# A decoder block's projections as seven half-matrix products per group instead of eight

## What is computed

```
h = rms_norm(x, g_mix)                                   # 256 x 1024
qa, ka, va, z, beta, a, qd, kd, vd, gate_a, gate_b = split(h @ w_in)   # mostly 1024 columns each
oa = gated_delta_rule(l2(silu(conv(qa))), l2(silu(conv(ka))), silu(conv(va)), ...)
oa = rms_norm(oa, g_delta_out) * silu(z)
od = rms_norm(diff_attention(rms(qd), rms(kd), vd, ...), g_subln) * (1 - lam_init)
x1 = x + (sigmoid(gate_a + b) * oa + sigmoid(gate_b + b) * od) @ w_o
out = x1 + experts(rms_norm(x1), top 4 of 32; w_up 1024 x 2048, w_down 1024 x 1024 each)
```

## Time and profile before

| | |
|---|---|
| median of 3 runs | 1276.09 us (1275.90 to 1276.17) |
| span of the profiled execution | 1273.7 us |
| PE busy | 1229.8 us, 97% |
| DVE busy | 373.2 us, 29% |
| ACT busy | 284.8 us, 22% |
| granted TensorE clock | 0.999 of full |
| moved by DMA | 451.94 MB, mean 355 GB/s |
| chain that ended last | PE 66%, DMA 19%, DVE 5%, ACT 3% |

### The profile page before, as it was taken

The page is one execution under the profiler, slowest core; times in us unless marked ns, Lnnn a source line. Parts: engine busy times, 40 slices in busy tenths (PEclk is TensorE's granted clock), DMA queues, the critical chain, the costliest instruction groups (busy, mean ns, idle before and its releaser), DMA issues.

```text
span 1273.7 us, 14917 instructions
## 1 busy us (share of the span) xinstructions
PE 1229.8 (97%) x5590; PEld 539.1 (42%) x5590; DVE 373.2 (29%) x1063; ACT 284.8 (22%) x573; POOL 45.9 (4%) x100
## 2 busy tenths in 40 slices
PE   9999999999999999999999999999998989999997
PEld 7777466644443333333333333333333333333332
DVE  5766825666231211111221111221111112211111
ACT  3331212352222121121121112121121211121121
POOL 4400000101000000000000000000000000000000
PEclk9999999999999999999999999999999999999999
DMA  7653431567779999999999999999999999999997
GB/s 255 181 164 129 147 134 67 181 248 264 274 284 417 425 429 429 429 428 430 429 428 427 429 428 428 428 429 429 429 428 428 428 428 429 429 429 429 428 427 314
DMA packets 60764, 451.94 MB, mean 355 GB/s; under 512 B 10600, under 2 KB 13800, under 8 KB 36032
## 3 DMA queue, kind: packets, MB, share of 16 engines
q1 hardware_dynamic: 59176, 447.44, 85.2%
q0 software_dynamic: 1120, 3.56, 1.0%
q10 hardware_dynamic: 440, 0.58, 0.1%
HBM read 449.21 MB, written 1.97 MB: 354 GB/s over the span
## 4 chain that ended last, share of the span: by engine, by line
PE 66%; DMA 19%; DVE 5%; ACT 3%; issue 1%; SPq 1%; DVEq 0%; ACTq 0%
PE pb L1719 20%; DMA space<-in_w_up_dram 19%; PE pb L1766 14%; PE pb L1430 11%; PE pb L1660 4%; PE pb L1420 3%; PE pb L1647 3%; PE pb L1574 2%; PE pb L1395 2%; PE pb L1654 1%; PE pb L1679 1%; DVE buf_a L1334 1%; DVE buf_a L1331 1%; DVE buf_a L1328 1%; ACT buf_a L898 1%
## 5 line engine op out<-in xcount | busy, mean ns | idle before, releaser
L1719 PE MATMUL pb<-space,buf_a 128*64 128x512 f32 x2048 | 460.4, 595 | 15.5 <-DMA space<-in_w_up_dram 15.4
L1719 PEld LDWEIGHTS pb<-space,buf_a 128*64 128x64 f32 x2048 | 146.1, 137 | 284.8 <-issue 257.3
L1766 PE MATMUL pb<-space 128*64 128x512 f32 x1024 | 227.1, 595 | 7.3 <-ACT space L905 7.3
L1328 DVE TENSOR_SCALAR buf_a<-pb 128x256 f32<-128x256 f32 x64 | 27.0, 421 | 686.7 <-PE pb L1719 686.7
L1430 PE MATMUL pb<-space 128*128 128x512 f32 x384 | 171.4, 594 | 0.0
L1766 PEld LDWEIGHTS pb<-space 128*64 128x64 f32 x1024 | 70.7, 137 | 140.9 <-issue 125.3
L1430 PEld LDWEIGHTS pb<-space 128*128 128x128 f32 x384 | 70.3, 190 | 76.1 <-issue 75.1
L881 ACT ACT_TABLE_LOAD x32 | 41.1, 1283 | 222.5 <-PE pb L1647 222.5
L1420 PE MATMUL pb<-space 128*128 128x256 f32 x384 | 88.6, 384 | 0.9 <-ACT space L734 0.5
L1420 PEld LDWEIGHTS pb<-space 128*128 128x128 f32 x384 | 71.3, 190 | 13.1 <-issue 2.4
L898 ACT ACTIVATE buf_a<-buf_a 128x256 f32<-128x256 f32 x64 | 26.7, 417 | 216.7 <-DVE buf_a L1328 216.7
(11 more groups left out here) (299 smaller groups left out, 807.3 us busy)
## 6 DMA issues: line engine op xcount, KB each, us to landing
space<-in_w_up_dram SPq DMA_DIRECT2D x127, 2048.0 KB, 25.7
space<-in_w_down_dram SPq DMA_DIRECT2D x61, 2048.0 KB, 24.2
space<-in_w_in_dram SPq DMA_DIRECT2D x17, 2048.0 KB, 8.0
space<-in_w_o_dram SPq DMA_DIRECT2D x2, 2048.0 KB, 11.9
space<-in_w_down_dram SPq DMA_DIRECT2D x4, 1024.0 KB, 27.3
space<-in_w_down_dram SPq DMA_DIRECT2D x4, 512.0 KB, 16.0
space<-in_w_up_dram SPq DMA_DIRECT2D x2, 1024.0 KB, 41.1
xt<-in_x_dram SPq DMA_DIRECT2D x2, 512.0 KB, 5.3
```

The source lines that it names most:

```text
L1328: v.tensor_scalar(glu[:, cols], pairs[:, :, 0], LIMIT, None, ALU.min).then_inc(s_glu, 1)
L1719: ins = mm(up_out(hf, n_), xg[:, c, :], up_columns(line, hf, n_), start=False, stop=(c == KC - 1), skip_group_check=True)
L1766: ins = mm(pb[64 * hf:64 * hf + 64, 2, :], actT[:, c // 4 * 2 + c % 2, hf_in, :], slot(m)[:, at_:at_ + 512], start=(c == 0), stop=(c == KC ...
```

## The change

Each of the six token-major groups is now one 2x2 block product: the two halves of the channels times the two token blocks on one side (A11, A12, A21, A22, parts of hT), the two halves of the channels by the two halves of the columns on the other (B11, B12, B21, B22, quarters of 512x512, 1 MB each). Seven products of four matmuls each ("units" P5, P1, P3, P6, P2, P7, P4) take the place of eight times four, 42 places instead of 48. Each unit has the same matmul shape as before.

- The four sums of A blocks are made once, by POOL, into the place of x (SA1 to SA4 in xt); x is loaded a second time near the end for the residual.
- Of the weight sums, T starts as B11 (load by SP), B12 is added by a DMA that POOL issues, then DVE adds B22 after P5 and B21 after P6, in place. T3 starts as B12, and B22 is added by a second DMA from POOL.
- Units share two PSUM banks; P3, P6 and P7 add to what stands in the bank. ACT (for the gates DVE, with the bias) copies after P5, P1, P3 and P7; DVE makes the four results after P6, P2, P7 and P4.
- The square of kd and of oa goes from POOL to ACT; the scaling of oa goes partly to ACT (`osc`), the gain product to DVE; `odn` is in two parts. Many steps have other places: `qt` 8 and 9 (were 9, 10), `nq` behind place 9 and so ahead of the last `sb` (was 10, behind it), `nk` 15 (16), `ktd` 16 and 17 (18, 19), heads from 18 on (20), `odn` 34 and 37 (39), `oan` 38 (41), `mt` 40 and 41 (both 46).
- Some semaphores are merged under new names.

```diff
+    UNITS = ("P5", "P1", "P3", "P6", "P2", "P7", "P4")
...
+    def quarter_place(g, q):
+
+        if q == "T":
+            return ((8, 0), (6, 1))[g % 2]
+        return {"B11": (8, 1), "B22": (9, 0), "B21": (9, 1), "T3": (6, 0)}[q]
...
-    put(9, ("qt", 0))
-    put(10, ("qt", 1), ("nq",))
+    put(8, ("qt", 0))
+    put(9, ("qt", 1), ("nq",))
...
-    put(15, ("y3", 0))
-    put(16, ("yt", 0), ("nk",))
-    put(17, ("s1",))
-    put(18, ("ks",), ("ktd", 0))
-    put(19, ("y1", 1), ("ktd", 1))
+    put(15, ("y3", 0), ("nk",))
+    put(16, ("yt", 0), ("ktd", 0))
+    put(17, ("s1",), ("ktd", 1))
+    put(18, ("ks",))
+    put(19, ("y1", 1))
...
-        put(20 + 2 * h, ("a1", h))
-        put(22 + 2 * h, ("aw", h))
-        put(23 + 2 * h, ("a2", h))
-        put(24 + 2 * h, ("a3", h))
+        put(18 + 2 * h, ("a1", h))
+        put(20 + 2 * h, ("aw", h))
+        put(21 + 2 * h, ("a2", h))
+        put(22 + 2 * h, ("a3", h))
+    put(34, ("odn", 0, 6))
+    put(37, ("odn", 6, 8))
+    put(38, ("oan",))
     for i in after:
         after[i].sort(key=lambda it: {"aw": 0, "a2": 0, "a1": 2}.get(it[0], 1))
-    put(46, ("mt", 0), ("mt", 1))
-    put(39, ("odn",))
-    put(41, ("oan",))
+    put(40, ("mt", 0))
+    put(41, ("mt", 1))
...
+        A11, A12, A21, A22 = (hT[:, 4 * k:4 * k + 4, P * b:P * b + P] for b in range(NB) for k in range(2))
+        SA1, SA2, SA3, SA4 = (xt[:, b, 512 * i:512 * i + 512].rearrange("p (c t) -> p c t", c=4) for b in range(NB) for i in range(2))
...
+        FACTORS = {"P5": (SA1, "T"), "P1": (A11, "B11"), "P3": (SA4, "B22"), "P6": (SA2, "T"), "P2": (A12, "B21"), "P7": (SA3, "T3"), "P4": (A22, "T")}
...
+        def bank_of(g, name):
+
+            return (g + U[name]) % 2
...
+            def load_quarter(g, q):
+
+                if g == 0:
+                    sp.wait_ge(s_pj, {"B11": 16, "B22": 20, "B21": 21}[q])
+                else:
+                    sp.wait_ge(s_pj, unit(g - 1, {"B11": "P1", "B22": "P3", "B21": "P2"}[q]))
+                    if q != "B11":
+                        sp.wait_ge(s_tadd, 2 * g - ("B21", "B22").index(q))
+                sp.dma_start(quarter_at(g, q), w_quarter(g, q)).then_inc(s_q(q), 16)
+
+            def begin_sum(g):
+
+                sp.wait_ge(s_pj, (16, 24)[g] if g < 2 else unit(g - 2, "P4"))
+                sp.dma_start(quarter_at(g, "T"), w_quarter(g, "B11")).then_inc(s_tb[g % 2], 16)
+
+            def begin_third_sum(g):
+
+                sp.wait_ge(s_pj, unit(g - 1, "P7") if g else 24)
+                sp.dma_start(quarter_at(g, "T3"), w_quarter(g, "B12")).then_inc(s_t3b, 16)
...
+            begin_third_sum(QD)
+            begin_sum(KD)
+            for q in ("B11", "B22", "B21"):
+                load_quarter(KD, q)
+            begin_third_sum(KD)
+            begin_sum(VD)
+            for q in ("B11", "B22"):
+                load_quarter(VD, q)
+
+            sp.wait_ge(s_tc, 1)
+            sp.dma_start(t_dram.ap(), Tc_f).then_inc(s_m32, 16)
+            sp.wait_ge(s_m32, 32)
+            sp.wait_ge(s_t0z, 1)
...
+            sp.wait_ge(s_pj, unit(GB, "P1"))
+            load_w_o(0, 0)
+            load_w_o(0, 1)
...
+            link(pool.tensor_tensor(SA1, A21, A22, ALU.subtract))
+            link(pool.tensor_tensor(SA2, SA1, A11, ALU.subtract))
+            pool.tensor_tensor(SA3, A11, A21, ALU.subtract).then_inc(s_hT, 1)
+            pool.tensor_tensor(SA4, A12, SA2, ALU.add).then_inc(s_hT, 1)
...
+            def grow(g):
+
+                pool.wait_ge(s_tb[g % 2], 16 * (g // 2 + 1))
+                pool.dma_start(quarter_at(g, "T"), w_quarter(g, "B12"), accum_op=ALU.add).then_inc(s_t[g % 2], 16)
+
+            def grow_third(g):
+                pool.wait_ge(s_t3b, 16 * (g + 1))
+                pool.dma_start(quarter_at(g, "T3"), w_quarter(g, "B22"), accum_op=ALU.add).then_inc(s_t3, 16)
+
+            grow(QD)
+            grow_third(QD)
+            grow(KD)
...
+                elif it[0] == "u":
+                    g, name = it[1], UNITS[it[2]]
+                    if name in COPIED and g < GA:
+                        k = COPIED[name]
+                        act_e.wait_ge(s_pj, unit(g, name))
+                        if name == "P5" and g == VD:
+                            act_e.wait_ge(s_psA, nA[("vt", 1)] + 1)
+                        elif name == "P5" and g == Z:
+                            act_e.wait_ge(s_red, 2)
+                        sc.copy(group_out(g, k), pb[:, bank_of(g, name), :]).then_inc(s_pjf, 1)
+                    if g == GB and name in LAST_USED:
+                        use(g, LAST_USED[name])
+                    elif g < GB and name in USED:
+                        use(g, USED[name])
+                    if name == "P5" and g:
+                        use(g - 1, 3)
...
+            def take_with_bias(g, name, k):
+
+                bias_ = gbias[:, g - GA, 512 * OUTS[k][1]:512 * OUTS[k][1] + 512]
+                dve.wait_ge(s_pj, unit(g, name))
+                if g == GB:
+                    dve.wait_ge(s_gm, 4 + k + 1)
+                v.tensor_tensor(gate_out[k], pb[:, bank_of(g, name), :], bias_, ALU.add).then_inc(s_pjf, 1)
+
+            def grow(g, name, q):
+
+                dve.wait_ge(s_pj, unit(g, name))
+                dve.wait_ge(s_q(q), loaded(g, q))
+                v.tensor_tensor(quarter(g, "T"), quarter(g, "T"), quarter(g, q), ALU.add).then_inc(s_tadd, 1)
+
+            def group_result(g, name):
+
+                k = RESULT[name]
+                dst, src = group_out(g, k), pb[:, bank_of(g, name), :]
+                dve.wait_ge(s_pj, unit(g, name))
+                if name == "P6":
+                    dve.wait_ge(s_pjf, copied(g, 3))
+                    ins = v.tensor_tensor(dst, dst, src, ALU.subtract)
+                elif name == "P2":
+                    dve.wait_ge(s_pjf, copied(g, 2))
+                    ins = v.tensor_tensor(dst, src, dst, ALU.add)
+                elif name == "P7":
+                    if g < GA:
+                        dve.wait_ge(s_pjf, copied(g, 4))
+                        src = group_out(g, 3)
+                    ins = v.tensor_tensor(dst, dst, src, ALU.subtract)
+                else:
+                    dve.wait_ge(s_pjf, copied(g, 4))
+                    ins = v.tensor_tensor(dst, src, dst, ALU.add)
+                ins.then_inc(s_cf, 1)
+
+            RESULT = {"P6": 0, "P2": 1, "P7": 2, "P4": 3}
+            COPIED = {"P5": 2, "P1": 1, "P3": 0, "P7": 3}
...
+                    for b in range(NB):
+                        ins = v.tensor_tensor(OA[:, b], OA[:, b], gz[:, b], ALU.mult)
+                    link(ins)
+                elif it[0] == "u":
+                    g, name = it[1], UNITS[it[2]]
+                    if g > Z and name == "P5":
+                        gate_product(g - 1, 2)
+                    if name in RESULT:
+                        group_result(g, name)
+                    if g >= GA and name in COPIED:
+                        if g == GA and name == "P5":
+                            dve.wait_ge(s_ml, 64)
+                        take_with_bias(g, name, COPIED[name])
+                    if name == "P5":
+                        grow(g, name, "B22")
+                    elif name == "P6":
+                        grow(g, name, "B21")
+                    if g > Z and name == "P1":
+                        gate_product(g - 1, 3)
+                    elif g >= Z and name == "P7":
+                        gate_product(g, 0)
+                    elif g >= Z and name == "P4":
+                        gate_product(g, 1)
+                        if g == GB:
+                            gate_product(g, 2)
+                            gate_product(g, 3)
...
+                elif it[0] == "u":
+                    g, name = it[1], UNITS[it[2]]
+                    rows, q = FACTORS[name]
+                    bank = bank_of(g, name)
+                    if name == "P5":
+                        if g == 0:
+                            pe.wait_ge(s_pjf, 23)
+                            pe.wait_ge(s_hT, 4)
+                        else:
+                            pe.wait_ge(s_pjf, copied(g - 1, 4))
+                        pe.wait_ge(s_t[g % 2], 16 * (g // 2 + 1))
+                    elif name == "P1":
+                        if g == 0:
+                            pe.wait_ge(s_pjf, 24)
+                        else:
+                            pe.wait_ge(s_cf, 4 * g)
+                        pe.wait_ge(s_q(q), loaded(g, q))
+                    elif name == "P3":
+                        pe.wait_ge(s_pjf, copied(g, 1))
+                        pe.wait_ge(s_q(q), loaded(g, q))
+                    elif name == "P6":
+                        pe.wait_ge(s_pjf, copied(g, 2))
+                        pe.wait_ge(s_tadd, 2 * g + 1)
+                    elif name == "P2":
+                        pe.wait_ge(s_pjf, copied(g, 3))
+                        pe.wait_ge(s_q(q), loaded(g, q))
```

(22 more changed lines are left out.)

355 lines of the change are left out of this document (187 added, 168 removed).

## The result

The changed kernel takes 1300.97 us (median of 4 runs, 1296.16 to 1301.88) beside 1276.13 us for the kernel before (1275.9 to 1276.45): ratio 1.0184, 95% interval 1.0167 to 1.0201. The direction was right; the size was not: +24.8 us instead of +10, outside the stated 1273 to 1297. The profiled execution has a span of 1299.3 us, 25.6 more than the one before.

A forecast was written before the change was run, and what follows sets the result against it. PE was taken to bound the kernel until 921.8 us, then the DMA of w_up. Terms -20.6 + 14.5 + 1.6 + 0.3 + 6.3 + 8.2 = +10.3 us on 1276.1 gave 1286 us, range 1273 to 1297.

The forecast's parts named there:

- What goes: PE's products in the six groups: 48 halves become 42 units of 3.44 us, 20.6 us less on PE.
- Term 1: Before the first n2: DVE's added work ends the inverse's elimination late, at 167.2 us, and PE stands 14.5 us.
- Term 2: The second root, nk, moved earlier: PE arrives 1.6 us too early, and 0.3 more at the second transpose.
- Term 3: Attention units: DVE's and ACT's steps for the heads come late beside sums and results, +6.3 us, bounds 0 to 12.
- Term 4: End of the mix: PE waits for DVE and ACT around the first turns and P3, +8.2 us, bounds 4 to 12.
- POOL's four sums of hT: Beside the first stretch's tiles: cost nothing, at worst 5 us of DVE's slack between tiles.
- I take 7: nothing: Accumulating loads for the weight sums: 7 us to landing assumed, so no wait; at 15 us the sum gains 4.9.
- rival D: Accumulating loads take 15 us or more, third sums late, +4.9 us, 1291 us; chance 8%.
- the clock as a rival: PE's clock drops in the stall at n2, about 5 us more, 1291 us; chance 14%.
- One for one: Expert stretch: the end moves by as much as the experts' start; pairs keep 54.8 and 58.7 us.
- The rival that DVE's sums fit (A): Sums fit DVE's gaps, the inverse is late only by the moved root: -5.7 us, 1270 us; chance 17%.

The follow-up runs named there:

- b_sums: The kernel before plus only POOL's four sums of hT, into a buffer nothing reads: 1281.24 us.
- a_plain: The changed kernel with its accumulating loads as plain loads on the same queue, the sums they form left out: 1297.17 us.
- a_t3: The changed kernel with the first and the accumulating load of Q's third weight sum issued ahead of the m blocks' stores: 1295.83 us.
- a_nosum: The changed kernel without three of DVE's weight-block additions ahead of n2, that computation left out: 1295.76 us.
- comb6: comb4 with q's norm one unit later, first mix transposes behind the last unit, delta scaling one unit earlier, six heads' root one unit later: 1268.39 us.
- comb4: The changed kernel with the edits of a_spread, a_t3 (K's first load too), a_later3, l3_front, q's norm behind the elimination, gating two units earlier: 1280.57 us.
- a_later3: The changed kernel with the delta rule's chain, from n2 to the scaling of its results, three units later: 1298.77 us.
- l3_front: a_later3 with the first expert slab's load issued behind GB's second block, no longer ahead of GA's third: 1290.16 us.
- a_spread: The changed kernel with POOL's four sums of hT some 10 us later, one at a time behind projection tiles 14 to 17: 1294.06 us.
- a_awake: The changed kernel with 54 products that nothing reads in PE's wait ahead of the first n2: 1299.68 us.
- c4_nq: comb4 with the norm of q one unit later still: 1275.63 us.

## Why the prediction was wrong, by its steps

- **What goes, -20.6 us.** Right: 336 records, eight from start to start in 3.43 us (159.53 to 162.96).
- **Term 1, n2, +14.5.** Right in kind and size at its place: 12.74 us, sums at 2.28 and results at 0.69 against 2.2 and 0.69 taken. The elimination ended 10 us later than forecast (177.4, not 167.2), because it inherited 5.7 us from the tiles and 4.24 us of a wait for ACT's copy of the late P7, which the prediction didn't have. PE was delayed by the same causes, so it stood no longer for it.
- **Term 2, +1.9.** Measured 1.39, at the same transpose.
- **Term 3, attention, +6.3.** 1.33 + 1.91 + 2.51 = 5.75, at the heads and on the engines named. The forecast had taken off 0.5 for the kernel before; the trace has 0.63 there, so like for like it is 5.1.
- **Term 4, the end, +8.2.** 4.08 + 2.11 + 0.77 + 0.82 = 7.8.
- **Failed: "POOL's four sums of hT fall ... beside the tiles of the first stretch: nothing, and at worst 5 us of DVE's slack between tiles."** DVE had no such slack: the stretched step stood ahead of the work that frees PE's banks, PE's wait rose from 0.48 to 3.91 us and its clock fell for a tile, 2.62 us more. b_sums shows it alone: 5.3 us in all. This step stood at nothing in the sum.
- **Failed: "I take 7: nothing"** for accumulating loads. 12.5 us from issue (130.61) to PE's start at P7, 11.1 in the median; PE waited 3.10 us. The window that it had to fit was forecast rightly: from POOL's issue to P7's need 9.4 us (124.5 to 133.9) in the prediction, 9.3 (130.61 to 139.90) in the trace, both ends later by what the tiles lost. Only the load's time was wrong: 12.5 us against 7 taken, so PE stood the difference to the window. a_plain and a_t3 show it. It is rival D's kind (8%), but short of its 15 us.
- **Failed: the clock as a rival.** It was given 14% and one place, and stood at nothing in the sum. It is not a case beside the forecast but a charge that came with four of the waits (3.91, 3.10, 12.74 and 4.08 us): 9.7 us, 2.67 of them at n2 (5 were estimated). Behind the waits of 1.91 and 2.51 us it stayed. The prediction had the rule of the Trainium skill at hand ("TensorE: Matmul & The Clock Gate", Part 1: the gate closes on an idle array and opens only after sustained work); the trace agrees with a clock of 0.67 to 0.76 behind these four waits, and it should have stood in the sum.
- **One for one.** Right within 1.1 us.

The sum with what was measured: 10.3 + 3.4 + 3.1 + 9.7, and 3.2 less in terms 1 to 4, is 23.3; with the experts' 1.1 it is 24.4 of 25.6. Of the other 1.2, 0.48 is a wait for DVE at a transpose near 128 us that every changed kernel has and b_sums has not. The way of counting explains the rest to 0.2 us: a unit is 3.60 us by itself but 3.43 from start to start, so each of some nine waits costs 0.16 more than its bracket says, less the 0.63 that PE waited before and 0.3 by which the tiles began earlier. The range was too narrow because three prices that no row showed were each taken at the end where nothing happens.

The rival that DVE's sums fit (A) was wrong for this order of the queues: without three of the sums n2 comes 4.6 us earlier (a_nosum), and term 3 came nearly as forecast. That comb6 comes to 1268.39, near A's 1270, with every sum in place, is no proof of A: comb6 has the chain three units later, which A did not suppose.

## What to carry to other kernels

When work moves from the engine that bounds to one that is a third busy, the price here was less the amount than each place where the added step stands ahead of something the bounding engine waits for: list those places, and price each wait with the clock that it costs. Before moving a chain later, look in every transfer queue for a load that waits for the chain's end, and for what is queued behind it. Parts don't add exactly: the edits in comb4 gained 25.4 us one by one in the medians (a_later3 counted with l3_front) and 20.4 together; the last three gained 9.7 alone and 12.2 together. No single edit brought the median of the changed kernel below 1294 us.

## What the runs showed of the hardware

- DVE's steps on SBUF stood still beside POOL's additions of two SBUF tensors (128x512, 1.27 to 1.44 us): three steps of 1.52 us together took 4.25 and 4.18, one of 0.42 took 1.37, and the last of them ended 0.3 us after POOL's last sum beside it. This is what the Trainium skill says ("SBUF — State Buffer", "Who interferes with whom": a VectorE instruction whose two inputs are both in SBUF contends with a GpSimd instruction that reads SBUF); the traces agree with it for the steps with two inputs. A step of 0.35 us with one tensor input was held too: 1.06 in the changed kernel, 1.12 in a_spread (74.61 us, beside POOL's sum at 74.31). In b_sums the same step took 0.35: it began between two of POOL's sums. Read before the prediction, the rule would have pointed at the first stage.
- An accumulating load into SBUF of 1 MB takes 11.1 us where a plain one takes 6.8 on the same queue. The DMA engines are as full (share 1.08 and 1.04 from 128 to 144 us), but move less (312 and 387 GB/s). Throughput in forty slices of that stretch, changed kernel and then a_plain:

```profile
GB/s 384 384 389 389 384 389 389 379 394 384 394 374 389 389 399 369 379 292 200 205 241 256 271 236 266 282 256 266 241 266 282 251 266 246 266 277 287 236 266 282
```

```profile
GB/s 384 399 384 343 394 394 399 374 404 389 389 384 399 389 379 389 440 389 358 410 364 430 323 415 389 369 384 415 379 379 394 384 399 353 415 353 369 394 399 384
```

- A short wait may cost the clock or not: behind 3.10 us the unit took 5.37, behind 3.19 (a_nosum) and 3.02 (a_awake) at the same place 3.67; behind 2.42 (comb6) one took 5.40, behind 2.51 (changed kernel) none was slower. What decides, these runs don't show. Kernels with such waits scatter, and their clock with them: the changed kernel's fastest execution of four, 1296.16 us, has a granted clock of 0.993, the others, 1300.87 to 1301.88, 0.987 to 0.988. c4_nq's ten fall into five of 1273.4 to 1274.6 at 0.998 to 0.999 and five of 1276.7 to 1278.5 at 0.994 to 0.996. The kernel before stays within 2.1 us over 26 executions on the same chip, and comb6 within 2.1 over five, both at 0.999 to 1.000.
